# Triangular inversion in a hybrid encoder: levels below 64 as two 64x64 diagonal blocks instead of one 128x128 matrix

## The reference

```python
def _chunk_gated_delta(q, k, v, g, beta):
    ...
    L = jnp.where(strict, jnp.einsum("...id,...jd->...ij", kb, k) * decay, 0.0)
    sol = lax.linalg.triangular_solve(eye + L, rhs, left_side=True, lower=True, unit_diagonal=True)
    ...
# RWKV-7, token by token (in chunks it needs the same kind of solve)
def step(S, inp):
    r_t, w_t, k_t, v_t, a_t, b_t = inp
    sa = jnp.einsum("dbhij,dbhj->dbhi", S, a_t)
    S = S * w_t[..., None, :] + sa[..., :, None] * b_t[..., None, :] + v_t[..., :, None] * k_t[..., None, :]
    return S, jnp.einsum("dbhij,dbhj->dbhi", S, r_t)
```

## Time and profile before

| | |
|---|---|
| runs | 3327.88 us median of 3 (3312.94, 3327.88, 3331.92) |
| profiled execution, span of its instructions | 3333.3 us |
| TensorE busy | 3222.5 us (97%) |
| VectorE, ScalarE, GpSimd busy | 2135.0, 1682.0, 610.8 us |
| mean granted TensorE clock | 0.972 of full speed |
| RWKV pairs of the two layers, from first to last inversion | 355 to 532 us, 1998 to 2178 us |
| the three DeltaNet inversions of the first layer | from 576.85, 656.09 and 735.02 us on |

### The profile page before, as it was taken

How to read it: one execution, slowest core, us unless ns; L and a number is a source line. 1 busy time by engine, 2 the same in 40 slices (tenths; PEclk the granted TensorE clock), 3 DMA queues, 4 the chain that set the end, 5 groups by cost and what they waited for, 6 DMA issues and landing times.

```text
span 3333.3 us, 51588 instructions
## 1 busy us (share of the span) xinstructions
PE 3222.5 (97%) x18431; PEld 2802.3 (84%) x18431; DVE 2135.0 (64%) x3426; ACT 1682.0 (50%) x2659; POOL 610.8 (18%) x521
## 2 busy tenths in 40 slices
PE   8999998999999999999999999999999999999998
PEld 7899897877888888888788998887878888888886
DVE  5775655776677777545568655556767777774554
ACT  5545544444655555444455565434455555554444
POOL 2000442342122212100000013324411222220000
PEclk9999997999999999999999998979999999999999
DMA  6666001113566666665556650011145665656654
GB/s 204 180 181 180 25 1 32 49 58 95 172 194 193 188 183 193 223 194 189 166 167 193 188 149 1 1 51 57 52 124 177 192 189 178 187 191 219 192 185 153
DMA packets 265208, 478.91 MB, mean 144 GB/s; under 512 B 17314, under 2 KB 81148, under 8 KB 264380
## 3 DMA queue, kind: packets, MB, share of 16 engines
q1 hardware_dynamic: 265020, 476.48, 46.4%
HBM read 474.32 MB, written 2.10 MB: 143 GB/s over the span
## 4 chain that ended last, share of the span: by engine, by line
PE 90%; DVE 5%; ACT 2%; issue 1%; DVEq 0%; ACTq 0%; POOL 0%; SPq 0%; DMA 0%; POOLq 0%
PE ps L625 89%; PE ps L629 1%; ACT L1223 1%; DVE wlo L1727 1%; DVE upair L1740 0%; ACT UA L1223 0%; DVE H L1759 0%; DVE AR L2128 0%; ACT XS L1223 0%; DVE TN L2149 0%; DVE TN L1786 0%; DVE rf L2163 0%; POOL H L562 0%; ACT whi L1223 0%; DVE XS L1776 0%
## 5 line engine op out<-in xcount | busy, mean ns | idle before, releaser
L1727 DVE TENSOR_TENSOR wlo<-ring,whi 128x1024 fp32r<-128x1024 f32 (+4 forms) x905 | 1086.3, 1217 | 693.8 <-ACT whi L1223 687.3
L625 PE MATMUL ps<-upair,whi 128*128 128x512 f32 x4032 | 1416.9, 396 | 5.8 <-DVE upair L1740 5.2
L1223 ACT ACTIVATE whi<-ring 128x1024 fp32r<-128x1024 f32 (+4 forms) x947 | 941.1, 1002 | 805.3 <-PE ps L625 752.8
L625 PE MATMUL ps<-upair,wlo 128*128 128x256 f32 x4032 | 1130.9, 280 | 0.0
L625 PEld LDWEIGHTS ps<-upair,whi 128*128 128x128 f32 x4032 | 757.4, 188 | 186.1 <-issue 5.9
L625 PEld LDWEIGHTS ps<-upair,wlo 128*128 128x128 f32 x4032 | 762.7, 189 | 0.3 <-issue 0.2
L625 PE MATMUL ps<-whi,upair 128*128 128x390 f32 (+2 forms) x1280 | 367.9, 364 | 0.0
L607 POOL TENSOR_TENSOR YB<-YB 128x1024 f32<-128x1024 f32 x22 | 125.2, 5691 | 837.9 <-DVE YB L1750 837.9
L625 PE MATMUL ps<-whi,ghi 128*128 128x512 f32 x704 | 274.4, 390 | 0.0
L625 PE MATMUL ps<-whi,glo 128*128 128x512 f32 x704 | 274.0, 389 | 0.0
L625 PE MATMUL ps<-wlo,ghi 128*128 128x512 f32 x704 | 273.9, 389 | 0.0
(11 more groups left out here) (304 smaller groups left out, 3802.6 us busy)
## 6 DMA issues: line engine op xcount, KB each, us to landing
ring<-in_w_up_dram SPq DMA_DIRECT2D x352, 512.0 KB, 3.8
ring<-in_w_down_dram SPq DMA_DIRECT2D x176, 512.0 KB, 4.2
ring<-in_w_in_dram SPq DMA_DIRECT2D x128, 384.0 KB, 3.5
ring<-in_w_out_dram SPq DMA_DIRECT2D x64, 512.0 KB, 3.8
ring<-in_w_ple_gate_dram SPq DMA_DIRECT2D x64, 512.0 KB, 4.1
ring<-in_w_in_dram SPq DMA_DIRECT2D x51, 512.0 KB, 4.4
ring<-in_w_in_dram SPq DMA_DIRECT2D x64, 390.0 KB, 3.5
ring<-in_w_in_dram SPq DMA_DIRECT2D x32, 396.0 KB, 3.4
```

The source lines that it names most:

```text
L625: return pe.matmul(o_, a, b, start=start, stop=stop, skip_group_check=True)
L1223: return act.activation(o_, i_, f, **kw)
L1727: v.tensor_tensor(wlo[:, slot % RING, :, 0:w], ring[:, slot % RING, :, 0:w], whi[:, slot % RING, :, 0:w].bitcast(F32), SUB).then_inc(S["lo ...
```

## The change

Below block size 64 the inverse is block diagonal, with two 64x64 blocks. The changed kernel keeps only these two, one in partitions 0 to 63 and one in 64 to 127, over the same 64 columns. `TNb`, `TTb` and `XSb` are these packed forms; `TNb` and `TTb` are the two halves of the `TN` tile, `XSb` is in `XS`. Each 128x128x128 matmul of levels 0 to 4 becomes two 64x64x64 matmuls, one for each half of the rows, into the same half of PSUM's partitions of the same bank. Masks, products with masks, transposes and copies of these levels are 128x256 instead of 128x512. At level 4 the result is written to the full `TT` layout again, in two copies, one for each half; level 5 reads it, and its matmuls get 64 instead of 128 weight columns. The zero quarter of `TT` is set once a layer. The masks are built full size in the place of `TT` and copied.

```diff
@@ sizes and places
-        LEVELS = 7
-        lev = [sb(f"lev{d}", [P, LEVELS, P], BF16) for d in range(2)]
+        LEVELS, HB = 6, P // 2
+        lev = [sb(f"lev{d}", [P, LEVELS, HB], BF16) for d in range(2)]
...
+        lev_full = [at(f"lev_full{d}", [P, LEVELS, P], xs_place + 4 * 4 * P * d - 2 * 4 * 4 * P, BF16) for d in range(2)]
...
+        TNb, TTb = ([TN[d][:, 2 * i:2 * i + 2, :].rearrange("p a c -> p (a c)").rearrange("p (j c) -> p j c", c=HB)
+                     for d in range(2)] for i in range(2))
+        XSb = [XS[d][:, 0:2, :].rearrange("p a c -> p (a c)").rearrange("p (j c) -> p j c", c=HB) for d in range(2)]
...
-        LEV = LEVELS - 1
+        LEV = LEVELS
...
-        EARLY = (slice(0, P // 2), slice(P // 2, P))
+        EARLY = HALVES = (slice(0, HB), slice(HB, P))
@@ GpSimd: masks, once
-                    sel(lev[d][:, m, :], lev[d][:, m, :], ALU.not_equal, 0, [[-1, P]], 1, 1.0)
+                    sel(lev_full[d][:, m, :], lev_full[d][:, m, :], ALU.not_equal, 0, [[-1, P]], 1, 1.0)
+            pool.drain()
...
+            for d in range(2):
+                for half in HALVES:
+                    pool.tensor_copy(lev[d][half, :, :], lev_full[d][half, :, half])
             pool.drain().then_inc(S["masks"], 1)
@@ TensorE: invert
                         for j in range(4):
+                            cols = slice(HB * j, HB * j + HB)
                             if lv < LEV - 1:
-                                last = mm(ps[4 * d][:, j * P:(j + 1) * P], nt(d, j), TN[d][:, j, :], True, True)
+                                for half in HALVES:
+                                    last = mm(ps[4 * d][half, cols], nt(d, j)[half, half], TNb[d][half, j, :], True, True)
                             else:
-                                last = mm(ps[4 * d][:, 64 * j:64 * j + 64], nt(d, j)[E, :], TN[d][E, j, E], True, True)
+                                last = mm(ps[4 * d][F, cols], nt(d, j)[E, F], TNb[d][E, j, :], True, True)
...
                             for j in range(4):
-                                last = mm(ps[4 * d][E, 64 * j:64 * j + 64], TT[d][:, j, E], XS[d][:, j, E], True, True)
+                                last = mm(ps[4 * d][E, HB * j:HB * j + HB], TTb[d][E, j, :], XSb[d][E, j, :], True, True)
...
                             if lv < LEV - 1:
-                                last = mm(ps[4 * d + 2][:, j * P:(j + 1) * P], XS[d][:, j, :], TT[d][:, j, :], True, True)
+                                for half in HALVES:
+                                    last = mm(ps[4 * d + 2][half, cols], XSb[d][half, j, :], TTb[d][half, j, :], True, True)
                             else:
-                                last = mm(ps[4 * d + 2][:, 64 * j:64 * j + 64], XS[d][F, j, :], TT[d][F, j, F], True, True)
+                                last = mm(ps[4 * d + 2][E, cols], XSb[d][F, j, :], TT[d][F, j, F], True, True)
@@ ScalarE: t1
-                        if lv < LEV - 1:
-                            a(mono(TT[d][:, :, :], 4), ps[4 * d + 2][:, :], ACT.Copy).then_inc(S[f"inv_tt{d}"], 1)
+                        if lv < SMALL:
+                            last = a(mono(TTb[d]), ps[4 * d + 2][:, 0:2 * P], ACT.Copy)
+                        elif lv == SMALL:
+                            for half in HALVES:
+                                last = a(TT[d][half, :, half], third(ps[4 * d + 2][half, 0:2 * P], 4), ACT.Copy)
@@ VectorE: invert_start, invert, start of a layer's first mixer
-                v.tensor_tensor(TT[d][:, :, :], nt, bmid(lev[1 - d][:, 0, :], 4), MUL)
+                for half in HALVES:
+                    v.tensor_tensor(TTb[d][half, :, :], nt[half, :, half], bmid(lev[1 - d][half, 0, :], 4), MUL)
                 v.drain()
-                v.transpose(mono(TN[d][:, :, :], 4), mono(TT[d][:, :, :], 4)).then_inc(S["inv_tn1"], 1)
+                v.transpose(mono(TNb[d]), mono(TTb[d])).then_inc(S["inv_tn1"], 1)
...
-                            v.tensor_tensor(XS[d][:, :, :], third(ps[4 * d][:, :], 4), bmid(lev[d][:, lv + 1, :], 4), MUL)\
+                            v.tensor_tensor(XSb[d], third(ps[4 * d][:, 0:2 * P], 4), bmid(lev[d][:, lv + 1, :], 4), MUL)\
...
-                            v.transpose(mono(TN[d][:, :, :], 4), ps[4 * d + 2][:, :]).then_inc(S["inv_tn"], 1)
+                            v.transpose(mono(TNb[d]), ps[4 * d + 2][:, 0:2 * P]).then_inc(S["inv_tn"], 1)
                         elif lv == SMALL:
-                            v.tensor_copy(mono(TT[0][:, :, :], 4), ps[2][:, :]).then_inc(S["inv_th"], 1)
+                            for half in HALVES:
+                                last = v.tensor_copy(TT[0][half, :, half], third(ps[2][half, 0:2 * P], 4))
+                            last.then_inc(S["inv_th"], 1)
...
                 v.wait_ge(S["masks"], 1)
+                for d in range(2):
+                    v.memset(TT[d][LATE[d], :, EARLY[d]], 0.0)
```

More of the change, by code:

```diff
@@ L189, in trunk @@
         TT = [sb(f"TT{d}", [P, 4, P]) for d in range(2)]
+        xs_place = place
         XS = [sb(f"XS{d}", [P, 4, P]) for d in range(2)]
+        lev_full = [at(f"lev_full{d}", [P, LEVELS, P], xs_place + 4 * 4 * P * d - 2 * 4 * 4 * P, BF16) for d in range(2)]
+        TNb, TTb = ([TN[d][:, 2 * i:2 * i + 2, :].rearrange("p a c -> p (a c)").rearrange("p (j c) -> p j c", c=HB)
+                     for d in range(2)] for i in range(2))
+        XSb = [XS[d][:, 0:2, :].rearrange("p a c -> p (a c)").rearrange("p (j c) -> p j c", c=HB) for d in range(2)]
         AR = [at(f"AR{d}", [P, NT, 2, P], u_place + 4096 + 2048 * d) for d in range(2)]
@@ L463, in _ @@
                 for d in range(2):
-                    cols = lev[d][:, m, :].rearrange("p (n w) -> p n w", w=2 * b)
+                    cols = lev_full[d][:, m, :].rearrange("p (n w) -> p n w", w=2 * b)
                     early, late = (cols[:, :, 0:b], cols[:, :, b:2 * b])[::1 - 2 * d]
@@ L1298, in t1 @@
                             act.wait_ge(S["inv_q"], m2 + (d + 1))
-                            a(TN[d][EARLY[d], :, EARLY[d]], ps[4 * d][EARLY[d], 0:2 * P].rearrange("p (j c) -> p j c", j=4), ACT.Copy)\
+                            a(TNb[d][EARLY[d], :, :], third(ps[4 * d][EARLY[d], 0:2 * P], 4), ACT.Copy)\
                                 .then_inc(S["inv_tq"], 1)
@@ L1307, in t1 @@
                             act.wait_ge(S["inv_t"], ml + (2 * lv + d + 1))
-                        if lv < LEV - 1:
-                            a(mono(TT[d][:, :, :], 4), ps[4 * d + 2][:, :], ACT.Copy).then_inc(S[f"inv_tt{d}"], 1)
-                        else:
-                            a(TT[d][EARLY[d], :, LATE[d]], ps[4 * d + 2][EARLY[d], 0:2 * P].rearrange("p (j c) -> p j c", j=4), ACT.Copy)\
-                                .then_inc(S[f"inv_tt{d}"], 1)
+                        if lv < SMALL:
[3 more added lines that the diff above has]
+                                last = a(TT[d][half, :, half], third(ps[4 * d + 2][half, 0:2 * P], 4), ACT.Copy)
+                        else:
+                            last = a(TT[d][EARLY[d], :, LATE[d]], third(ps[4 * d + 2][EARLY[d], 0:2 * P], 4), ACT.Copy)
+                        last.then_inc(S[f"inv_tt{d}"], 1)
                     if between:
@@ L1775, in invert @@
                         if lv < LEV - 1:
-                            v.tensor_tensor(XS[d][:, :, :], third(ps[4 * d][:, :], 4), bmid(lev[d][:, lv + 1, :], 4), MUL)\
+                            v.tensor_tensor(XSb[d], third(ps[4 * d][:, 0:2 * P], 4), bmid(lev[d][:, lv + 1, :], 4), MUL)\
                                 .then_inc(S["inv_xs"], 1)
                         else:
-                            v.tensor_copy(XS[d][LATE[d], :, EARLY[d]], ps[4 * d][LATE[d], 0:2 * P].rearrange("p (j c) -> p j c", j=4))\
-                                .then_inc(S["inv_xs"], 1)
+                            v.tensor_copy(mono(XSb[d][LATE[d], :, :]), ps[4 * d][LATE[d], 0:2 * P]).then_inc(S["inv_xs"], 1)
                     for d in range(2):
@@ L1785, in invert @@
                         if lv < SMALL:
-                            v.transpose(mono(TN[d][:, :, :], 4), ps[4 * d + 2][:, :]).then_inc(S["inv_tn"], 1)
+                            v.transpose(mono(TNb[d]), ps[4 * d + 2][:, 0:2 * P]).then_inc(S["inv_tn"], 1)
                         elif lv == SMALL:
-                            v.tensor_copy(mono(TT[0][:, :, :], 4), ps[2][:, :]).then_inc(S["inv_th"], 1)
-                        else:
-                            v.tensor_copy(TT[0][EARLY[0], :, LATE[0]], ps[2][EARLY[0], 0:2 * P].rearrange("p (j c) -> p j c", j=4))\
-                                .then_inc(S["inv_th"], 1)
+                            for half in HALVES:
+                                last = v.tensor_copy(TT[0][half, :, half], third(ps[2][half, 0:2 * P], 4))
+                            last.then_inc(S["inv_th"], 1)
+                        else:
```

(1 more changed line is left out.)

1 line of the change is left out of this document (added).

## The result

| | before | changed |
|---|---|---|
| median of the runs beside each other | 3329.9 us (3312.94 to 3333.15) | 3231.66 us (3226.73 to 3234.43, 4 runs) |
| span of the profiled execution | 3333.3 us | 3229.7 us |
| TensorE busy | 3222.5 us | 3096.3 us |
| mean granted clock | 0.972 | 0.965 |

The ratio is 0.9715, with a 95% interval of 0.9689 to 0.9741: the change takes 98 us off, where 111 were forecast. Beside the experiments the changed kernel ran again: 3234.57 us against 3326.80, ratio 0.9722 (0.9700 to 0.9743).

What follows compares the result with a forecast made beforehand. TensorE was taken to bound the kernel, weight columns pacing its small float32 matmuls. RWKV 70 + DeltaNet 56 - clock 15 = 111 us off 3328 gave 3217 us; own range 3185 to 3255, wider range 3185 to 3300.

Steps and rivals of the forecast that it cites:

- T(0) to T(1): RWKV inversion, VectorE is the chain: shorter transpose 1.12 us and shorter product 0.27, saving 1.39 us.
- T(1) to the product of level 2: RWKV inversion, TensorE in order: three groups of 0.43 us less, saving 1.29 us.
- X(4) to Q: RWKV inversion, from level 4's first product to the next step: 1.98 us falls to 1.24, saving 0.74.
- The packed group and the level: One direction's matmuls 0.46 us instead of 0.89; a level 2.50 us instead of 3.91, bound by one direction's chain.
- the gain is used up by what stands beside the inversions: Rival: `rw_decays`, `ml_pair`, ScalarE's table loads and slots' operands end last; half the sum, 3270 us, chance 0.13.
- The DeltaNet inversions: Inversions of DeltaNet pairs, some work filled by output projection slots: 9.3 us saved each, six of them, 56 us.
- The clock: TensorE's gaps in packed levels bring more half-clock stretches: 15 us taken off the gain, RWKV stretch clock 0.80 to 0.90.
- The sum: Whole kernel: 70 us from RWKV and 56 from DeltaNet inversions, less 15 for clock, 111 us saved.
- The inversions' total: Whole kernel: inversions read as 14 stretches of 32 to 41 us, some 490 us of 3333.
- At nothing: Mask copies, clears and split copies of level 4 forecast to cost nothing, being covered; without cover 4 us in all.
- The slower rival: Clock falls to 1.2 GHz through most of the mixers: 3390 us, or 3400 without parallel halves; chance 0.09, both forms.
- One after the other: Rival: row halves sharing a PSUM bank take turns, a group stays at 0.93 us; 3298 us, chance 0.09.

Runs made afterwards that it cites:

- filled kernels: Useless 128x128 float32 matmuls put into TensorE's stops in RWKV inversions: changed kernel with six and eighteen 3211.86 us, kernel before with six and fourteen 3315.91 us.
- a variant that is worse by some 17 us at full clock: Changed kernel with VectorE's masked products and transposes 128x512 again, matmuls still packed: 3224.38 us, again 3224.14 us.
- one with more work: Changed kernel plus useless matmuls, six before T(1) in each RWKV inversion and eighteen before T(3) in a layer's last RWKV pair: 3211.86 us, again 3217.12 us.
- filled kernel before: Kernel before plus useless matmuls, six before T(1) in each RWKV inversion and fourteen before T(3) in a layer's last pair: 3315.91 us, ratio 0.9962.

## Why the prediction was right, point by point

The time was forecast at 3217 us and came out at 3231.66, within the range and its narrower one (3185 to 3255). The mechanism was the one forecast: the halves run beside each other, and a level is bound by the chain of one direction. The steps of an RWKV inversion are best held against one that ran wholly at full clock: that of the first layer's third pair in the kernel with twelve useless matmuls per DeltaNet pair (the six before T(1) lie within the stop there), whose window shows it.

```profile
431.80:456.00 24.20, 22.32 (x436) 19.58 (x435) 15.66 (x43) 17.95 (x47) 11.38 (x18) 1.00 0.01 3
```

| step | saved, forecast | measured at full clock |
|---|---|---|
| X(0) | 0.86 | 0.91 |
| T(0) to T(1) | 1.39 | 1.28 |
| T(1) to the product of level 2 | 1.29 | 1.02 |
| from there to X(3) | 0.98 | 1.01 |
| level 3 | 1.41 | 1.47 |
| X(4) to Q | 0.74 | 0.14 |
| Q, T(4), the values | 1.3 | 1.28 |
| X(5) and T(5) | 0.77 | 0.86 |
| sum | 8.7 | 8.0 |

- **The packed group and the level** were right to 0.06 us, 0.46 with the halves side by side against 0.93 one after the other included.
- **X(4) to Q is the step that was wrong.** It counted TensorE's group and VectorE's product, and not ScalarE's copies of level 3. In the timeline of the kernel before there are two of them, one for each direction. Q of the first direction waits for the first alone, which ends at 471.95, 0.9 us ahead of Q at 472.85:

```profile
471.34 1.09 ACT L1223 ACTIVATE TT<-ps 128x512 f32<-128x512 f32 x2
```

  With levels 2 and 3 shorter by 1.4 us each ScalarE ended last. It was named among the rivals ("the gain is used up by what stands beside the inversions"), and cost 0.55 us in six inversions, 3 us in all.
- **T(1) to the product of level 2** was forecast to shrink by 1.29. At full clock it shrank by 1.02; in the changed kernel as it is it grew, from 4.74 to 5.31 us (T(1) at 1998.09), for it runs at half clock. That belongs to the term for the clock.
- **The DeltaNet inversions** saved 8.6 us where one ran at full clock (44.3 to 35.7, at 698.10), of 9.3 forecast.
- **The clock** was forecast at 15 us. The half-clock time rose by 39 us (187 to 226), by 32 at most without the start of the kernel, a bound of 16; in the windows it rose by 24 and 32, which makes 12 and 16; the table's bounds differ by 20, and the whole times of the filled kernels say about 10. The size was right. So was the place in the main: the whole rise lies inside the inversions (43 us of half clock in them before, 78 after), and outside them in the windows there is none (116 and 113). But it doesn't stand in the gaps of the packed levels. In the RWKV pairs it stands from T(1) on, behind a stop that the kernel before had too, of 1.82 us and in two of four pairs with half clock behind it; now it is 2.03 us or more in six, all six with half clock. Another 14 us of the rise lie in the DeltaNet inversions (3 before, 17 after). The RWKV stretch's clock was 0.82 and 0.81, inside the 0.80 to 0.90.
- **The sum.** Of the 126 us forecast before the clock the inversions give 8 x 8.0 + 6 x 8.6 = 116 at full clock, and the windows 109, by their estimate without half clock. So 10 us of the miss are the inversions' steps, and some 7 more stand in the windows and have not been assigned. The whole times say 103 filled, or 112 by the bounds of the table ((3326.8 - 90) less (3234.57 - 110)). In the profiled pair 8 of the 104 us between the spans (3333.3 and 3229.7) are the kernel's end, 909 us before and 900 after, and so not the change's, by what the other profiles show.
- **The inversions' total** was read as some 490 us of lengths from 32 to 41. From X(0) to the first matmul that reads the result the 14 of the profile before last 32.1 to 46.1 us, 548 together. No term of the sum rests on it.
- **At nothing:** mask copies, clears and split copies left no wait in the rows looked at; they were not tried apart.
- **The slower rival** fell: it decided at a clock below 0.7, and the clock held at 0.81. Its mechanism is real but small. *One after the other* was forecast at 3298; with every matmul twice, which gives a group that length, the time was 3286 us, still faster than before. *The gain used up* has one true piece, Q's wait.

The mean inversion length in the two profiles fell by 6.7 us (RWKV, forecast 8.7) and 7.4 (DeltaNet, 9.3); the differences to the full-clock numbers, some 1.2 us each time, are the clock's share inside the inversions.

## What to carry to other kernels

Where the work of a chain of small float32 matmuls is block diagonal, alternate the halves of the rows: two 64x64x64 then took the time of one (0.43 us for eight, 0.46 for four in one half). Once a level is bound by the chain through VectorE and ScalarE, look up what the other engines have to end before the next step, and how far ahead they ended: 0.9 us was too little here. And a cut in TensorE's work is partly paid in clock: read the granted clock stretch by stretch before judging a variant, for here a variant that is worse by some 17 us at full clock measured as no worse, and one with more work was faster than both kernels (3211.86 us). Compare the stretch that was changed, too, and not the whole time alone.

## What was unexpected of the hardware

- After the same stop of 5.49 us before T(3), in one execution of the kernel with six useless matmuls, the clock stayed at half for 44.4 us in the first layer and 10.2 us in the second, with TensorE at work.
- Stretches of 13.65 us at half clock stand in the pairs' ends, with no stop in them, and none longer than 0.41 us in the 7 us ahead. TensorE is busy throughout, with the next pair's scores, the outputs' products and the next X(0) (window 387.70:401.40).
- The stretch from the last inversion of the first layer to the first of the second took 1217 us in most profiles and 1226 to 1227 in three, the one from the second layer's last inversion to the end of the kernel 900 or 909, whichever kernel it was.
- Eleven to seventeen runs of one kernel spread by 0.6 to 0.8%, and the shortest times tend to come with the higher mean clock (3301.29 us at 0.979, 3325.78 us at 0.973 in the filled kernel before).
